# Moving two weight casts and interleaving the gates at the seams of a two-block transformer kernel

## The reference, cut to what matters

```
h = h + 0.5 * swiglu(rmsnorm(h, ffn1_norm), ffn1_w_gu, ffn1_w_down)
u = rmsnorm(h, mix_norm)
... = split(u @ w_in)
merged = sigmoid(g_conv) * y_conv + sigmoid(g_mla) * y_mla
h = h + merged @ w_o
h = h + 0.5 * swiglu(rmsnorm(h, ffn2_norm), ffn2_w_gu, ffn2_w_down)
gate = sigmoid(rmsnorm(h, ple_norm) @ w_ple_gate)
h = h + gate * (p @ w_ple_proj)
```

## Time and profile before

| | before |
|---|---|
| median of 3 runs | 2003.04 us (2002.78 to 2004.69) |
| profiled execution, whole | 2002.78 us |
| its span, first to last instruction | 2000.9 us |
| TensorE matmul busy | 1928.5 us, 96% |
| VectorE busy | 1350.3 us, 67% |
| ScalarE busy | 996.6 us, 50% |
| GpSimd busy | 238.0 us, 12% |
| mean granted TensorE clock | 0.983 |

### The profile page before, as it was taken

One profiled execution on the slowest core, in us unless ns is written; L12 is line 12 of the kernel. 1 busy time (PEld: TensorE's weight loads), 2 busy tenths in 40 slices (PEclk: granted clock), 3 DMA queues, 4 the chain that ended last, 5 costly groups with the idle time before them and its releaser, 6 DMA issues.

```text
span 2000.9 us, 36557 instructions
## 1 busy us (share of the span) xinstructions
PE 1928.5 (96%) x15864; PEld 1910.4 (95%) x15864; DVE 1350.3 (67%) x1605; ACT 996.6 (50%) x1231; POOL 238.0 (12%) x168
## 2 busy tenths in 40 slices
PE   7999999999999999999999999988999998889998
PEld 7999999999999999999999999987999998789998
DVE  6655777775559555787785558886755688675556
ACT  5433545554347433545564336665433476653333
POOL 3000100010002000100010002472100026610000
PEclk9999999999999999999999999988999999799999
DMA  8555454465554555544555554413455543236551
GB/s 262 185 183 182 157 172 160 137 202 189 190 196 149 209 190 192 176 128 166 165 173 190 190 190 140 148 48 127 152 204 172 175 155 106 69 122 207 178 191 62
DMA packets 246531, 329.55 MB, mean 165 GB/s; under 512 B 6246, under 2 KB 218788, under 8 KB 246372
## 3 DMA queue, kind: packets, MB, share of 16 engines
q1 hardware_dynamic: 246018, 326.79, 49.1%
q10 hardware_dynamic: 258, 0.16, 0.1%
q0 software_dynamic: 96, 0.26, 0.0%
HBM read 326.14 MB, written 1.05 MB: 164 GB/s over the span
## 4 chain that ended last, share of the span: by engine, by line
PE 80%; DVE 12%; ACT 4%; POOL 2%; issue 1%; DMA 1%; ACTq 0%; POOLq 0%; DVEq 0%; SPq 0%
PE work L1982 18%; PE work L1983 18%; PE work L1984 18%; PE acc L1982 8%; PE acc L1984 8%; PE acc L1983 8%; DVE w_lo L1296 4%; ACT w_hi L796 1%; DVE ra L1309 1%; POOL fa L743 1%; POOL fa L717 1%; DVE fa L1730 1%; DVE fa L1341 1%; PE work L2109 1%; PE acc L2052 1%
## 5 line engine op out<-in xcount | busy, mean ns | idle before, releaser
L1982 PE MATMUL work<-xh,w_hi 128*128 128x256 f32 x2560 | 723.9, 283 | 23.9 <-DVE xl L1330 12.0
L1296 DVE TENSOR_TENSOR w_lo<-raw,w_hi 128x2048 fp32r<-128x2048 f32 (+2 forms) x314 | 706.6, 2260 | 44.3 <-ACT w_hi L796 42.0
L1983 PE MATMUL work<-xl,w_hi 128*128 128x256 f32 x2560 | 721.2, 282 | 0.0
L1984 PE MATMUL work<-xh,w_lo 128*128 128x256 f32 x2560 | 719.5, 281 | 0.0
L796 ACT ACTIVATE w_hi<-raw 128x2048 fp32r<-128x2048 f32 (+2 forms) x314 | 578.5, 1850 | 168.1 <-PE work L1984 82.7
L1982 PEld LDWEIGHTS work<-xh,w_hi 128*128 128x128 f32 x2560 | 485.1, 190 | 27.7 <-issue 24.4
L1983 PEld LDWEIGHTS work<-xl,w_hi 128*128 128x128 f32 x2560 | 485.7, 190 | 0.3
L1984 PEld LDWEIGHTS work<-xh,w_lo 128*128 128x128 f32 x2560 | 485.8, 190 | 0.0
L1341 DVE TENSOR_TENSOR fa<-work,rstd 128x512 f32<-128x512 f32 x168 | 115.1, 690 | 400.8 <-PE work L1984 400.2
L1982 PE MATMUL acc<-ra,w_hi 128*128 128x256 f32 x1344 | 377.8, 281 | 0.0
L1984 PE MATMUL acc<-ra,w_lo 128*128 128x256 f32 x1344 | 377.5, 281 | 0.0
(11 more groups left out here) (287 smaller groups left out, 2298.7 us busy)
## 6 DMA issues: line engine op xcount, KB each, us to landing
raw<-in_ffn_w_gu_dram SPq DMA_DIRECT2D x88, 1024.0 KB, 5.1
raw<-in_w_in_dram SPq DMA_DIRECT2D x52, 1024.0 KB, 5.4
raw<-in_ffn_w_down_dram SPq DMA_DIRECT2D x44, 1024.0 KB, 5.1
raw<-in_w_up_dram SPq DMA_DIRECT2D x32, 1024.0 KB, 5.6
raw<-in_w_down_dram SPq DMA_DIRECT2D x32, 1024.0 KB, 7.0
raw<-in_w_mla_out_dram SPq DMA_DIRECT2D x8, 1024.0 KB, 5.1
raw<-in_w_o_dram SPq DMA_DIRECT2D x8, 1024.0 KB, 5.1
raw<-in_w_ple_gate_dram SPq DMA_DIRECT2D x8, 1024.0 KB, 5.4
```

The lines of the kernel that those rows point to most:

```text
L1296: v.tensor_tensor(w_lo[:, s, 0:n], raw[:, r, 0:n], w_hi[:, s, 0:n].bitcast(F32), ALU.subtract).then_inc(lo_done.sem, 1)
L1982: pe.matmul(dst, ah, bh, start=start and i == 0, stop=False, skip_group_check=not group)
L1983: pe.matmul(dst, ah, bl, start=False, stop=False, skip_group_check=not group)
L1984: last = pe.matmul(dst, al, bh, start=False, stop=stop and i == len(pairs) - 1, skip_group_check=not group)
```

## The change

Three orders are changed; no instruction is added or taken away.

- Merge: ScalarE's cast of chunk W1+1 moves from before bank 0's copy to before bank 2's, and VectorE's low half of it from behind bank 0's add to behind bank 2's (and behind the low part of bank 1).
- End of the second feed-forward network: VectorE's low half of G1+1 moves ahead of all four banks, and the low parts `gl` of bank 0 and bank 1 come one bank later.
- Gates 2 and 3: VectorE and ScalarE take gate 2 through to its split (`next_layer(2)`) before gate 3 is begun. In the last layer ScalarE's cast of the chunk A2 moves ahead of `next_layer(2)`; the low half stays last on VectorE.

```diff
@@ ScalarE, merge
                 act.activation(smla, smla, ACT.Sigmoid).then_inc(act_out.event(here, "gmla"), 1)
-                next_hi(here, c + 1)
                 for b in range(NB):
+                    if b == 2:
+                        next_hi(here, c + 1)
                     if b == NB - 1:
                         conv_gate(3)
@@ ScalarE, gates
                 gate_sigmoid(2)
+                if layer == DEPTH - 1:
+                    next_hi(here, G1 + 3)
+                next_layer(2)
                 gate_sigmoid(3)
-                next_layer(2)
                 next_layer(3)
-                next_hi(here, G1 + 3)
+                if layer < DEPTH - 1:
+                    next_hi(here, G1 + 3)
@@ VectorE, end of a feed-forward network
-                last = f + (33 if use == 2 else 32)
+                last = f + 32
+                if use == 2:
+                    next_lo(here, f + 32)
+                    last += 1
                 for b in range(NB):
                     v.wait_ge(acc_done.sem, acc_done.after(here, use * NB + b))
                     v.scalar_tensor_tensor(h[:, 2 * b:2 * b + 2, :], acc[:, b, :].rearrange("p (a t) -> p a t", a=2), 0.5,
                                            h[:, 2 * b:2 * b + 2, :], ALU.mult, ALU.add).then_inc(acc_taken.sem, 1)
-                    if use == 2 and b == 0:
-                        next_lo(here, f + 32)
-                        norm_lo(here, *following, banks=(0,), x=x)
-                    elif b > (1 if use == 2 else 0):
+                    if b:
                         norm_lo(here, *following, banks=(b - 1,), x=x)
@@ VectorE, merge
                     if 0 < b < NB - 1:
                         merged_lo(b - 1)
-                    if b == 0:
+                    if b == 2:
                         next_lo(here, c + 1)
@@ VectorE, gates
-                gate_in(2)
-                gate_in(3)
-                gated(2)
-                gated(3)
-                next_layer(2)
-                next_layer(3)
+                for i in range(2, 4):
+                    gate_in(i)
+                    gated(i)
+                    next_layer(i)
                 next_lo(here, G1 + 3)
```

## The result

The changed kernel takes 2012.89 us, median of 5 runs (2011.92 to 2015.04), against 2003.04 (2001.23 to 2004.69) before: 9.85 us more. The ratio is 1.0054 with a 95% interval of 1.0042 to 1.0065, or 8.4 to 13.0 us. It is above the 1.0049 of these two medians: the record has fourteen executions of the changed kernel in all, with a median of 2013.6. The change is slower by more than the 0.2% named in the prediction, and inside its range of 2006.6 to 2013.9; the forecast was 2011.1.

What follows compares the result with a forecast made beforehand. TensorE, busy 96% of the span, was taken as the bound, so only its waits move the end. Merge 3.8, layer 0 with the FFN end 3.2 and last layer 1.3 sum to 8.3 on 2002.78: 2011.1 us, range 2006.6 to 2013.9.

Steps and rivals of the forecast that it cites:

- Part 1: Merge, once a layer: W1+1's low half comes late and TensorE starts the W1 pair 1.9 us later; two layers +3.8 us.
- Part 2: End of second FFN, twice: the pair on G1 starts 0.8 us later, the reciprocal and what follows on VectorE 0.7 later.
- Part 3: Gates, first layer: gate 3 pays a second round trip, so F1+2 comes late; +3.2 us including the second FFN's end.
- Part 4: Gates, last layer: gate 3's later round trip delays A2's low half, so TensorE gets A2 late; +1.3 us.
- By that rule A2's low half, which starts ahead of the fold, is not slowed at all (+1.3 stands): Last layer's gates: under the exclusive SBUF lock the later instruction blocks, so +1.3; by the slower reading +2.1 us.
- That A2's high half is early gains nothing: Last layer's gates: ScalarE's early cast of A2 brings no gain, since the low half waits for VectorE.
- The gates win what the merge loses: Rival: TensorE's gate-stage waits, up to 5.3 us, go and outweigh the merge's 3.8; 2001.3 us, chance 0.04.
- The gate stages come out even: Rival: the second round trip hides behind TensorE's eight steps, only the merge is paid; 2006.6 us, chance 0.10.
- The merge is swallowed: Rival: a later wait absorbs the merge's delay, only the gates are paid; 2007.3 us, chance 0.06.
- The clock falls: Rival: TensorE's clock drops after its waits before bank 3 and A2, 1.4 us a stretch; 2012.5 to 2014, chance 0.2.

Runs made afterwards that it cites:

- merge_low_at_bank1: Kernel before with only VectorE's low half of W1+1 moved from behind bank 0 to behind bank 1: 2002.61 us, ratio 1.0000.
- merge_low_at_bank2: Kernel before with only VectorE's low half of W1+1 moved behind bank 2, ScalarE's cast where it was: 2009.24 us, ratio 1.0036.
- merge_only: Kernel before with the change's merge edits alone, on ScalarE and VectorE, in both layers: 2009.28 us, ratio 1.0030.
- merge_first_layer: Kernel before with the merge edits in the first layer only, the second layer's merge and cast as before: 2005.95 us, ratio 1.0016.
- gates_only: Kernel before with the change's gate edits alone on both engines, including ScalarE's early cast of A2: 2005.72 us, ratio 1.0013.
- gates_cast_late: Same as gates_only, but ScalarE casts A2 last in the last layer, as in the kernel before: 2008.63 us, ratio 1.0029.
- ffn_end_and_gates: Kernel before with the edits at the end of the second FFN and at the gates, without the merge edits: 2006.40 us, ratio 1.0021.
- ffn_end_only: Kernel before with the change's edits at the end of the second FFN alone: 2005.02 us, ratio 1.0013.

## Why the prediction was right, and where it was not

**Part 1, the merge: the wait right, the price too small.** Forecast 1.9 a layer, measured 1.94; the walk's 386.7 for the low half was 387.2 in an execution that ran 0.5 us late from its start. merge_low_at_bank1 and merge_low_at_bank2 show that the slack of 2.1 us is what decides: a low half that starts 1.8 us later costs nothing (2.54 before the pair instead of 4.37), one that starts some 3.9 later costs 1.9. What was mis-sized is the term "Two layers: **+3.8 us**". merge_only measured 6.8, and merge_first_layer half of that. The waits in it are 3.9. The new wait is followed by some 16 matmuls in 3 us in five cases of seven, each 1.5 us, which is 2.1 us for two merges on average. Some 0.8 are left; the intervals are wider than that.

**Part 2, the end of the second FFN: too small by 0.3.** Forecast +0.8 at G1 and +0.7 from there on; measured +1.05 at G1 and +1.0 at F1 (2.53 less the clock's 1.48, and -0.04). VectorE waited 0.35 for the standard deviation: the chain hung on TensorE's sum there, as the prediction said of the reciprocal, but then took only 0.7.

**Part 3, the gates in layer 0: right.** The sum with part 2 was forecast as 3.2 and is 1.01 + 2.37 = 3.4 (both from the profile of the changed kernel). Bank 3's wait was forecast as about 0.9 and is 0.86.

**Part 4, the last layer: 1.3 forecast, 2.4 measured** (1.12 of W1 to QK without the clock's 1.5, 0.40 and 0.89). Beside part 2's share that is 1.3 where 0.6 was forecast, and two steps of it failed. "By that rule A2's low half, which starts ahead of the fold, is not slowed at all (+1.3 stands)" is right for the low half, which took 2.29 us, but it looked at one side of the lock only: what is blocked then is GpSimd. Its two last steps each wait for a low half, the second low half waits for the first of them and takes 3.36, and the sum of squares comes only when they end:

```profile
1260.20 2.29 DVE L1300 TENSOR_TENSOR w_lo<-raw,w_hi 128x2048 fp32r<-128x2048 f32 x1
1262.40 3.36 DVE L1300 TENSOR_TENSOR w_lo<-raw,w_hi 128x2048 fp32r<-128x2048 f32 x1
```

In gates_only TensorE stood idle 0.7 us for it. In the changed kernel's profile it worked through the same time at half clock, so the fold's end and the slow matmuls each account for the 0.89; gates_only, with full clock there and +0.90, shows that the fold alone suffices. And "That A2's high half is early gains nothing" was wrong: in the new order the cast would come after bank 3's squares, VectorE would wait 2.12 for it, and gates_cast_late shows 2.3 us at A2, 2.9 in all. The prediction's 0.25 for what the early cast costs looked at bank 2 only. The early cast is what kept the last layer's price down.

**The sum.** The stretches of the profile, without the two clock falls behind the merges, add up to 2.0 + 1.9 for the merges, 3.4 for layer 0 and 2.4 for the last layer, 9.7 against 8.3 forecast. The median of five moved 9.85, that of all fourteen 10.6. The nearness is in part luck. By the single experiments the merge costs 3.0 more than its term (6.8 against 3.8), and the rest 0.8 less than its terms (3.7 for ffn_end_and_gates against 4.5), so two errors of opposite sign are in the total. The medians of the three single parts, 6.8 + 2.5 + 3.1, make 12.4, those of merge_only and ffn_end_and_gates 10.5, both with the clock in them. With two parts the sum agrees with the whole; with three it is some 2 us above it, and each of them is uncertain by about as much. Where the difference goes is not settled; from sum to the end the profiles of these kernels differ by up to 3.3 us (-2.05 to +1.26) with the same instructions.

**The rivals.** "The gates win what the merge loses" fell: the waits for `xl` in the last layer grew from 2.0 to 3.4. Its ground was sound, though: the four `xl` shrink from 4.25 to 1.67 once the fold is away, and in the last layer 2.7 us were to be had. It took the early cast and a low half moved out of the fold's way, and not a second round trip. "The gate stages come out even" fell with +2.37 for F1 to F1+2, and "The merge is swallowed" with merge_only, where the 1.93 lost at W1 is not made up by G1 (216.95 as before). "The clock falls", with its chance of 0.2, was right that the clock would fall and in part about the place: it fell behind bank 3's wait in the changed kernel and in ffn_end_and_gates, not in gates_only, and there it was covered by the fold. Where it cost 1.5 us a time, behind the merges, the prediction had not looked.

## What to carry to other kernels

A weight cast can be moved back for free only as far as the first matmul that waits for its low half. Measure that slack first: 2.1 us here, of which 1.8 could be used and 3.9 not. Finishing one tile before the next is begun pays the hand-over between two engines twice (2.3 and 1.4 us more in the two gate stages here); interleave instead, and use idle time of the second engine for casts that have no other input. When an operand moves ahead, follow what it now stands beside: twice a faster A2 was given back to the fold, until the next low half was moved as well.

## What the runs showed of the hardware

- A wait of TensorE of 1.9 us in the middle of dense work (27 matmuls in 3 us, clock 1.00) was followed by a stretch at half the clock, 1.2 GHz, in five of seven cases (some 16 matmuls in 3 us), at the cost of 1.5 us each; in two it was not, and at the same places without the wait it never was, in 17 cases. Behind A2, after waits of 1.6, 0.3 and 1.6 us, it fell in three profiles of six. A short wait can so cost nearly twice its length, and one profile doesn't tell which.
- GpSimd's adds in SBUF and VectorE's subtractions with two SBUF inputs exclude each other. One 512-column add takes 1.29 alone and 2.93 behind a low half; two in a row took 2.67 with VectorE idle, 4.42 behind one low half and 6.33 beside two. That is the exclusive lock of the Trainium skill, "SBUF — State Buffer", section "Who interferes with whom", and here the trace agrees to a few tenths: the first step of the 6.33 starts 0.39 us after the first low half has begun and has to wait for its end, and the second has to let the next low half pass.
